# Two kinds of expert loop, a different order at the layer ends, and a split overflow tile in a two-layer mixture-of-experts kernel

## The reference

```
for every token: best group of 4 (of 16 experts), then the top 2 experts inside it, gates = softmax of the two logits
y = sum over the two experts e of gate[e] * (silu(x @ w_gate[e]) * (x @ w_up[e])) @ w_down[e]      # 1024 -> 512 -> 1024
x = layer_norm(alpha * x + y)
```

## Time and profile before

| | |
|---|---|
| median of 3 runs | 1619.08 us (1608.86 to 1638.03) |
| the profiled execution | 1626.72 us, of which its slowest core's span is 1625.6 us |
| cores | 1553.8 to 1625.6 us; core 4 is the slowest |
| PE busy on core 4 | 78% of the span (DVE 61%, ACT 45%, POOL 13%) |

### The profile page before, as it was taken

One profiled execution on the slowest core, in us unless ns is written; L12 is line 12 of the kernel. 1 busy time (PEld: TensorE's weight loads), 2 busy tenths in 40 slices (PEclk: granted clock), 3 DMA queues, 4 the chain that ended last, 5 costly groups with the idle time before them and its releaser, 6 DMA issues.

```text
span 1625.6 us, 34234 instructions; the slowest of 8 cores (1553.8 to 1625.6 us)
## 1 busy us (share of the span) xinstructions
PE 1267.5 (78%) x11706; PEld 829.5 (51%) x11706; DVE 985.4 (61%) x2553; ACT 730.2 (45%) x1449; POOL 214.1 (13%) x396
## 2 busy tenths in 40 slices
PE   3797796979739987888628986898963898889783
PEld 2543333445537766677424442444553676658563
DVE  1667476576735756566713774868683475745766
ACT  4555345444433453543244554545453244443533
POOL 4001101102100111111140110010110011110101
PEclk9898898989869998999858998999995999989897
DMA  9798999999746997998966786799744699956571
GB/s 180 214 321 114 134 152 120 144 117 134 205 156 135 215 230 193 209 241 172 184 156 126 130 111 135 96 158 115 130 170 157 119 215 230 243 146 166 163 158 52
DMA packets 64134, 266.08 MB, mean 164 GB/s; under 512 B 9008, under 2 KB 9648, under 8 KB 53936
## 3 DMA queue, kind: packets, MB, share of 16 engines
q0 software_dynamic: 34736, 147.84, 57.5%
q1 hardware_dynamic: 29184, 115.53, 22.2%
HBM read 327.08 MB, written 109.18 MB: 268 GB/s over the span
## 4 chain that ended last, share of the span: by engine, by line
PE 56%; DMA 14%; issue 11%; DVE 10%; ACT 7%; SPq 0%; POOL 0%; DVEq 0%; ACTq 0%; POOLq 0%
PE ps L625 34%; PE ps L1680 18%; DMA s_x<-x 3%; PE ps L628 3%; DMA s_k<-bw 3%; DMA s_x<-x_rows 2%; DVE s_x L667 2%; DMA s_x<-xs_rows 2%; DMA s_f<-gmwT 2%; DMA xs_rows<-s_x,s_sloti 2%; ACT s_f L641 2%; DVE s_sm L684 1%; DVE s_r L654 1%; ACT s_k L673 1%; ACT s_b L641 1%
## 5 line engine op out<-in xcount | busy, mean ns | idle before, releaser
L1680 PE MATMUL ps<-s_k 128*128 128x128 bf16 x6144 | 377.1, 223 | 35.0 <-issue 15.5
L1680 PEld LDWEIGHTS ps<-s_k 128*128 128x128 bf16 x6144 | 363.8, 100 | 55.8 <-issue 41.6
L625 PE MATMUL ps<-s_k,s_y 128*128 128x512 bf16 x1296 | 313.2, 389 | 35.5 <-DVE s_y L654 20.3
L625 PE MATMUL ps<-s_k 128*128 128x512 bf16 (+2 forms) x1400 | 281.4, 354 | 17.7 <-DMA s_k<-w_in 7.5
L641 ACT ACT_TABLE_LOAD x96 | 123.2, 1283 | 295.0 <-PE ps L1680 187.2
L625 PEld LDWEIGHTS ps<-s_k,s_y 128*128 128x128 bf16 x1296 | 123.3, 99 | 189.0 <-issue 71.6
L667 DVE SCALAR_TENSOR_TENSOR s_x<-s_x,s_sm,s_lp 128x1024 f32<-128x1024 f32 x162 | 203.7, 1275 | 10.9 <-ACT s_sm L641 7.9
L625 PEld LDWEIGHTS ps<-s_k 128*128 128x128 bf16 x1400 | 127.7, 105 | 130.5 <-issue 49.2
L667 DVE SCALAR_TENSOR_TENSOR s_x<-ps,s_x 128x512 f32<-128x512 f32 x192 | 140.5, 745 | 87.6 <-PE ps L625 64.5
L628 PE MATMUL ps<-s_identb,s_b 128*128 128x128 bf16 x920 | 87.6, 248 | 127.0 <-ACT s_b L673 59.9
L628 PEld LDWEIGHTS ps<-s_identb,s_b 128*128 128x128 bf16 x920 | 76.4, 152 | 145.6 <-issue 141.5
(11 more groups left out here) (160 smaller groups left out, 1239.7 us busy)
## 6 DMA issues: line engine op xcount, KB each, us to landing
s_k<-bw SPq DMA_DIRECT2D x48, 1024.0 KB, 12.4
s_x<-xs_rows SPq DMA_DIRECT2D x48, 514.0 KB, 10.6
bw<-exp_w_gate POOLq DMA_DIRECT2D x16, 1024.0 KB, 27.3
bw<-exp_w_up POOLq DMA_DIRECT2D x16, 1024.0 KB, 27.0
bw<-exp_w_down POOLq DMA_DIRECT2D x16, 1024.0 KB
s_k<-exp_w_gate POOLq DMA_DIRECT2D x16, 1024.0 KB, 13.5
s_k<-exp_w_up POOLq DMA_DIRECT2D x16, 1024.0 KB, 11.6
s_k<-exp_w_down POOLq DMA_DIRECT2D x16, 1024.0 KB, 16.6
```

Of the source, the lines that this page charges most:

```text
L625: pg.add(PE, lambda e: e.matmul(out.ap, lhsT.ap, rhs.ap, start=start, stop=stop), [out], [lhsT, rhs], d)
L1680: pg.add(PE, lambda en, o=o, lt=lt, rv=rv, kc=kc: en.matmul(o.ap, lt.ap, rv.ap, start=kc == 0, stop=kc == 7), [o], [lt, rv], 128 / 2.2e3)
```

## The change

1. Only a group's first expert (`e4 == 0`) and the layer's last, (3, 3), keep the tile-by-tile form. The other 11 of a layer's 16 take the form with 384 columns.
2. `behind` is a new list of an operation: it is scheduled behind these, without waiting for their results. In the last expert the third tile's gate and up matmuls are put behind the first tile's down matmuls, and the spill region behind the last scatter.
3. From the second layer on, the fourth piece of `w_in` waits for the last scatter of the layer before (as `w_o` did), ahead of `w_o`, with the `None` of the stream in front of it.
4. Pair 0 is finished behind the group's second expert, pairs 3 and 1 behind the third.
5. The overflow tile's parts are cut finer: the 12 small gate operations of `cast` come behind the transposes, and `store` becomes four regions (statistics and index on DVE, Ln and Exp on ACT, two passes on DVE, the scatter on POOL), so that other work of DVE may stand between them.

```diff
-                if True:
+                if e4 == 0 or (g, e4) == (3, 3):
+                    ends = []
...
+                                    if n == 2 and then:
+                                        pg.ops[-1].behind = ends[:1]
...
                         down(n, k, n * 512, 128)
+                        ends.append([o for o in pg.ops[-12:] if o.E is PE][-1])
...
+                    if e4 == 1:
+                        finish(g, (0,), cur)
                     if e4 == 2:
-                        finish(g, (0, 3, 1), cur)
+                        finish(g, (3, 1), cur)
...
             after = [o for o in pg.ops if o.kind == "d" and o.E is POOL][-1:]
-            spill_region(l, lw)
+            spill_region(l, lw, after)
...
-                dma(POOL, t().v(halves), halves(w_in_d[l, c]), [t()], [], 128 * 4096 * 4)
+                dma(POOL, t().v(halves), halves(w_in_d[l, c]), [t()], [], 128 * 4096 * 4, deps=lw.odeps if c == 3 else ())
...
             for c in range(4):
+                if l and c == 3:
+                    stream.append(None)
...
             want_w_in(l, lw)
-            stream.append(None)
+            if l == 0:
+                stream.append(None)
             want_w_o(l, lw)
```

In `schedule`, what `behind` does:

```diff
-            preds = {q.idx: q for q in o.deps}
+            preds = {q.idx: q for q in o.deps + o.behind}
...
             for q in o.succ:
+                if o.kind == "d" and o in q.behind:
+                    q.ready = max(q.ready, s + dur)
+                    q.npred -= 1
+                    if q.npred == 0:
+                        ready[q.E.name].append(q)
+                    continue
```

And in the overflow tile's store:

```diff
-                    C.do(ACT, lambda e: e.activation(out=go(23, 24).ap, in_=go(21, 22).ap, func=AF.Ln, bias=epsl().ap), [go], [go])
-                    C.do(ACT, lambda e: e.activation(out=go(23, 24).ap, in_=go(23, 24).ap, func=AF.Exp, scale=-0.5), [go], [go])
...
+                part(fn, [go], [xo(), cst(), lw.gcn()], [DVE], DVE)
...
+                part(fn1, [go(23, 24)], [go(8, 22), epsl()], [ACT], DVE)
+                pg.ops[-1].lag = 4.0 if g < 3 else 0.5
...
+                part(fn2, [xo], [go(), lw.ln2()], [DVE], DVE)
+                pg.ops[-1].lag = 3.0 if g < 3 else 0.0
...
+                part(fn3, [xo, go, (OUTD if l == L - 1 else SOD)(24 + g, 25 + g)], [ZD()], [POOL], POOL)
```

More of the change, by code:

```diff
@@ L170 @@
     __slots__ = ("E", "fn", "w", "r", "dur", "idx", "npred", "succ", "ready", "kind", "nbytes", "newt", "tiles", "tab",
-                 "end", "prio", "engs", "deps", "sk", "val", "lag")
+                 "end", "prio", "engs", "deps", "behind", "sk", "val", "lag")
 class Eng:
@@ L245, in add @@
         o.deps = list(deps)
+        o.behind = []
         o.succ = []
@@ L1101, in spill_region @@
             pg.region(body, w, r, pg.engs, 1.0)
+            pg.ops[-1].behind = behind
         def group_overflow(l, lw, g):
@@ L1114, in body @@
                     return done(E)
-                pg.region(body, [t() for t in w], r, engs, 0.25, E)
+                pg.region(body, [t if isinstance(t, Ref) else t() for t in w], r, engs, 0.25, E)
             def load():
@@ L1155, in flip, with fn3 @@
                 part(fn2, [to], [pt(), xb()], [DVE], DVE)
+                def fn3():
+                    V = lambda f, w_, r_: C.do(DVE, f, w_, r_)
+                    V(lambda e: e.tensor_scalar(out=go(8, 14).ap, in0=cst(300 + 6 * g, 306 + 6 * g).ap,
+                                                scalar1=xo(D + 3, D + 4).ap, scalar2=None, op0=ALU.is_equal), [go], [xo])
+                    V(lambda e: e.memset(go(0, 4).ap, 0.0), [go], [])
+                    for k, (a, c) in enumerate(PAIRS):
+                        for ee, m in ((a, D), (c, D + 1)):
+                            V(lambda e, ee=ee, m=m, k=k: e.scalar_tensor_tensor(
+                                out=go(ee, ee + 1).ap, in0=go(8 + k, 9 + k).ap, scalar=xo(m, m + 1).ap,
+                                in1=go(ee, ee + 1).ap, op0=ALU.mult, op1=ALU.add), [go], [xo, go])
+                part(fn3, [go], [xo(), cst()], [DVE], DVE)
             def up(e4, w):
```

34 lines of the change are left out of this document (12 added, 22 removed).

## The result

The changed kernel takes 1627.55 us (median of 20, 1620.12 to 1719.4) against 1619.89 us of the kernel before in the same comparison; the ratio is 1.0082 (95% interval 1.0058 to 1.0107). The two medians above are over all 20 executions of each kernel and would give 1.0047. The forecast was 1589, range 1564 to 1614. So the kernel is "same" by the 2% bound, but outside the range and on the other side of the kernel before.

The account below looks back on a forecast made before the run. PE was taken to bound the MoEs, DMA close behind in the first, and a chain the layer ends. Terms -7.5 - 6 - 8 - 6 - 8 + 3 = -32.5, 2.5 given back: -30 us, 1589 on the median, range 1564 to 1614.

Parts of the forecast that it names:

- the sum of the middle: 384-column form in both MoEs: -6 for faster matmuls, -8 for issue gaps, +3 us for the fourth slice.
- the two MoE parts, together 641.6 us: Core 4's two MoE stretches, 325.50 and 316.10 us, read as bound by PE, with DMA close behind in the first.
- Pace: 384-column form, 22 experts: one matmul of 384 columns at 166.5 ns beats three of 128 at 170.0; -6 us.
- Issue gaps: PE in the MoEs: longer matmuls queued ahead of a branch cover late instructions, half of 15.5 us goes; -8.
- The fourth slice: 384-column experts: all three tiles' down products wait for the fourth slice's product; +3 us, bounds -7 and +32.
- "Nothing" for the tables: Eight further `finish` calls: at most sixteen ACT table loads of 1.28 us cost nothing beyond the +3; bare, up to 20.
- rival A: 384-column experts: the wait for the fourth slice takes the gain back, slower; about 1618 at the +32 bound; chance 0.10.
- DVE busy with a pass: up to 1.28 us more: Fourth slice's product: a DVE pass over 1024 columns may delay it by up to 1.28 us, 22 times.
- The last expert: Ends of the two layers: first tile's products to last scatter, 37.00 to 26.5 us (-10.5) and 33.10 to 26 (-7).
- `w_in`: Between the layers: the late fourth piece shares DMA with the next tiles; +3 us, bounds 0 and +7.
- Overflow tile: Cores 4 and 2: cutting and spreading takes 4 us off the 4.78 and 4 off the 9.27 us stops; -8.
- Rivals B to D: B: middle gives nothing, 1598, chance 0.27. C: all issue gaps go, 1571, 0.15. D: late `w_in` costs 7, 1600, 0.05.

Follow-up runs that it names:

- t1_after_lag: The changed kernel with one planner's number changed, a pair tile's load planned to land 7 us later: 0.9835 of the kernel before (wide 0.990).
- o5_ovf: The kernel before with change 5 alone, the overflow tile's regions cut finer: 0.9880 of the kernel before (three executions).
- u4_finish: The changed kernel with change 4 undone, pairs 0, 3 and 1 finished together behind the third expert: 1.0064 of the kernel before.

## Why the prediction was wrong, point by point

**The term that failed** is "the sum of the middle": I took the 384-column form at -6 (pace) -8 (issue gaps) +3 (fourth slice and tables) = -11 us, and change 4 at nothing but table loads. Measured, the stretch ahead of the last down product grew by 20 and 18 us on the ordinary cores. The step that failed is to price each change by its own instructions and add: it had no term for the new order of the queues. One reading of the rows was off as well: "the two MoE parts, together 641.6 us" leaves out the first 34.8 us of the second MoE (they are 676.4), which moves none of the terms. By its parts:

- *Pace, -6.* PE's busy time in the first MoE stayed (283.29 and 283.39 on core 4, 280.70 and 283.35 on core 3): 2211 matmuls for 3640 on core 4, and no time gained, beside a granted clock of 0.91 instead of 0.96. I had priced the matmuls at the full-speed rows and not asked at which clock they would run. Where the waits went (t1_after_lag, clock 0.94 and 0.96) core 3's PE is busy 278.83 and 274.79 us, 1.9 and 4.7 less than before.
- *Issue gaps, -8.* Right as a mechanism and too small: in the first MoE of core 4 they went from 11.8 to under 1 us, and the form alone does it (18.4 to 1.7 and 16.0 to 6.3 on core 0). The Trainium skill says that a taken branch to a target outside the two loaded pages forces a fetch ("Runtime: NRT & Kernel Launch", "Instruction fetch mechanics"); from it I had a sum in which the gaps only move to other branches. They did not: the six cores have 0.0 us of them in the first MoE for 16.3, and 5.3 in the second for 14.6. That the longer queue of work ahead covers them fits this, and is not shown apart from it.
- *The fourth slice, +3, and "Nothing" for the tables.* This comes nearest to rival A, which I gave 0.10 and priced from the waits on `s_y` alone; its sign was right, its mechanism was not. The waits on `s_y` did stay small (13.4 us in all on core 4 for 20.3). The delays came at the other inputs: casts of the next tiles, one silu, marks. The step "DVE busy with a pass: up to 1.28 us more" bounded only engines that work. It had no term for an engine that stands, for 12 to 14 us, in its own queue, on a load.
- *Change 4.* I looked only at what `finish` does itself. It also frees a tile buffer one expert earlier; the next group's load and all that hangs on it move up with it. Alone it is the worst change, 1.0195 (wide 1.011). I should have asked of the freed buffer "what does it start, and who stands behind it in a queue": the row was there to see in the issue table, 10.6 us to landing.
- *The last expert, -10.5 and -7.* Measured -7.6 and -5.4 on core 4, so the chain I described holds; I missed the 6.01 and 5.35 us for which the third tile's down products wait behind other work of DVE.
- *`w_in`, +3.* From the last scatter to the first block of 512 on core 4: 861.34 - 822.52 = 38.8 before, 871.94 - 829.73 = 42.2 after: +3.4. The size fits on this core, partly by luck: on the six ordinary cores the step grew from 32.7 to 38.9 us, undoing change 3 in the changed kernel gives 4 back, and beside change 5 undone it gives 11, more than the bound of 7.
- *Overflow tile, -8.* For the filled tile itself the size is about right, alone and in company: cores 2 and 4 spend 36.8 us more in the second MoE than the ordinary cores in the kernel before, 32.1 in o5_ovf, 27.8 in the changed kernel and 36.5 in it without change 5 (means of the two cores). What is wrong is that every core pays for it in company: the changed kernel without change 5 is 18 us shorter in its ordinary cores' MoEs. Rivals B to D had the changes add up in the same way, so none of them came near.

**What is shown and what is not.** Shown: the changes do not add; the loss lies in PE's waits in the MoEs and in the clock behind them; change 4 costs alone and beside changes 2 and 5; late pair tiles in ACT's and DVE's queues cause single waits of 5 to 11 us of PE; undoing change 5 or planning those loads 7 us longer takes the loss away. The second brings most of the forecast gain by its ratio (0.9835; the forecast was 0.9816) and over half of it by the wide one (0.990), but by another path than the forecast's, so the nearness to its number is luck. Not shown: that the tiles are the whole cause. Undoing change 5 took the loss away with the tile stops as large as ever, the same planner's number makes the kernel before 2.9% slower, and u4_finish, which removes the early finish, gained nothing in sum. What the number took off the ordinary cores' MoEs is 49 us in the changed kernel and 33 with changes 1 and 5 (both with the form); in kernels with every expert tile by tile it is 28 (change 4 alone), 2 (the changed kernel without the form), -4 (changes 2 and 5) and -29 (before). So it helps where the form is and beside change 4 alone, and does nothing or harm elsewhere. A rival that I did not test is the landing itself: the two late tiles took 13.3 and 24.7 us to land, and nothing here says what they would have cost had their load been quick. My reading, argued and not shown: the form puts all of an expert's down products behind its last slice, so that PE has nothing else to issue when ACT or DVE stands; there punctual queues decide, and elsewhere a later plan only pushes work onto marks and weight loads. How much of each of the other differences is chance of the list scheduler stays open; the two layers of u4_finish, -7.4 and +7.4 us with one code, say that it can be 7 us a layer.

## What to carry to other kernels

When a planner orders the queues, a change's price is not its own instructions but the new order: compare for each engine what stands ahead of critical work and on which load it waits, and check the planner's load times against the issue table. Then measure, since a truer load time made one program here faster and another slower. A buffer freed earlier is not a gain if what it starts is queued in order ahead of present work. Measure changes in pairs before adding their prices, and price matmuls at the clock that the stretch will have, not at that of its best row.

Two versions are candidates to keep, and the runs do not separate them: the changed kernel with the pair tiles' loads planned 7 us later (0.9835, wide 0.990) and the kernel before with change 5 alone (0.988, wide 0.987). The first has the shorter MoEs by 23 us and two things still to plan: PE of core 2 stands 20.48 us ahead of its overflow tile's transposes, and the late piece of `w_in` sits between the layers.

## What the runs showed of the hardware

- ACT loads a table more often than its functions change. A load of 1.28 us stands between a Ln and its Exp (555.60 above) and between two silus (558.92). In the first MoE of core 4 the kernel before has 56 loads, of which 38 stand where the function before and behind belong together; change 5 alone (o5_ovf) has 63 and 45, the changed kernel 76 and 42. ACT's own branches are 21 in all three, so the loads that change 5 adds do not follow branches of ACT. That they follow the regions of other engines fits the numbers and is not shown. ACT is busy 167 us in the changed kernel's first MoE for 136.
- A wait of PE can cost twice. Behind waits of 5.74 and 4.32 us the next 20 down products took 344 ns each, at full speed 222. The granted clock (third figure from the end of a row) was full (2.4 GHz) ahead of the waits and 0.65 over the 6.4 us behind them, so PE spent most of these at the lower level, 1.2 GHz:

```profile
539.00:549.00 10.00, 10.00 (x64) 5.85 (x61) 3.16 (x7) 1.82 (x7) 0.00 (x0) 1.00 1.01 181
561.00:567.40 6.40, 6.40 (x23) 2.46 (x22) 4.06 (x7) 0.00 (x0) 1.01 (x1) 0.65 0.52 165
```

- In the first MoE of core 4, with a DMA share of 0.81, the loads of one pair tile (0.53 MB) took 5.6 to 28.8 us from issue to landing, 14.7 in the median (before: 9.1 to 22.7, median 14.7).
